# A two-block network on one core: attention's evictions reordered, the third norm's first tile on another engine, the norm's first chunks handed over singly

## The chip, the cores and the metric

One Trainium2 chip, of which the kernel uses one core. The metric is the device time in microseconds of one execution, the median of several. TensorE (PE) multiplies matrices out of SBUF into PSUM; VectorE (DVE), ScalarE (ACT) and GpSimd (POOL) work elementwise; SyncE (SP) issues most of the DMAs. Each engine runs its own instructions in order and meets the others at semaphores.

## The reference

The input is 256 tokens of width 1024, in float32. The first block has two layers. The first layer mixes with gated linear attention and an RWKV-7 recurrence, the second with latent attention (MLA) of 16 heads. Each layer ends in a feed-forward network, and each sublayer in a post-norm, so there are four layer norms. A second block follows, in which a condition vector modulates scales and shifts:

```python
def swiglu_ffn(x, w_gate_up, w_down):
    gu = x @ w_gate_up
    gate, up = gu[..., :FFN_HIDDEN], gu[..., FFN_HIDDEN:]
    return (jax.nn.silu(gate) * up) @ w_down

def layer_norm(x, g, b):
    xf = x.astype(jnp.float32)
    mu = xf.mean(-1, keepdims=True)
    var = jnp.square(xf - mu).mean(-1, keepdims=True)
    return ((xf - mu) * lax.rsqrt(var + LN_EPS) * g + b).astype(x.dtype)
```

The second block normalizes the rows by RMS, scales and shifts them by the modulation (a product of SiLU(c) with a 1024 by 6144 matrix), projects to queries, keys and values, attends with sinks and a relative bias (16 heads), adds a gated output, normalizes again, and ends with a 4096-wide squared-ReLU network.

## The kernel before

**Products.** Every large product is done with both factors split in a high and a low half (`mm3`, lines 443 to 446): high by high, high by low, low by high, three TensorE passes that accumulate in one PSUM bank.

**Weights.** All weight matrices are cut into pieces of up to 1 MB, in the order of their use (`pieces`). SyncE loads piece i into ring buffer i mod 3 as soon as piece i - 3 has left it (`sp_piece`, L434). ScalarE writes a piece's high half (`act_split`, L387), then VectorE the low half (`dve_split`, L400), which also frees the ring buffer. Split pieces go to three slots of their own; `ahead` says how far the splits run ahead of TensorE, two pieces. Among the pieces of the two feed-forward layers lie 24 of the modulation matrix (`w_ada`). TensorE doesn't use these: VectorE multiplies them with SiLU(c) and sums (`dve_modulation_piece`, L1738 and L1741), within `dve_split`, in the ring's order, and frees the buffer. The first such piece of a layer waits for the SiLU of c, which ScalarE does in `act_modulation_start` (L1718).

**Feed-forward.** `pe_ffn`, `act_ffn` and `dve_ffn` go over j = 0, 2, ..., 20, with two pieces each, g = 0 (gate) and g = 1 (up). The ring's order at the start of layer l is (j 0, g 0), (0, 1), modulation piece, (2, 0), (2, 1), modulation piece, (4, 0), (4, 1), modulation piece, and so on. The piece (0, 0) is split during the norm ahead. ScalarE's work in round j = 0 is the splits up to (2, 0) for g = 0, up to (2, 1) for g = 1, then the gate's SiLU.

**Norms.** Behind each norm TensorE transposes the two row tiles of XN into four banks, each with two chunks of 128 columns (`pe_transposed`, L532). VectorE scales and shifts the banks 0 and 2 (`dve_scaled`, L594 or L596), ScalarE the banks 1 and 3 (`act_scaled`, L571 or L573). ScalarE writes the high halves to XH (L581), VectorE the low halves to XL (L602), always for two chunks together. This happens six times: behind norms 0, 1 and 2, behind the RMS norm of MLA's compressed rows (tag cq), and for m0 and m1, the two modulated inputs of the second block. The consumers are `pe_pair` (first piece of a feed-forward layer and of w1) and `pe_rows` (min, mqb and va2).

**Norm 3** stands between the blocks. For row tile 0 `dve_residual` makes the statistics, `act_residual` normalizes to XN, and `pool_third` multiplies by the gain and adds the shift on GpSimd (L2318, L2322). For tile 1 `dve_third` does it all on VectorE (L2330, L2336). Then comes the RMS norm for m0 (`act_rms`, `dve_rms`).

**Attention.** `pe_attend`, `act_attend` and `dve_attend` run a pipeline over the heads with index i; head h = i - 3 is weighted in round i. In a round ScalarE first moves a finished group's output out of PSUM (L2158, every fourth head), then in MLA copies the turned queries and keys of an even head (L2163), then moves the transposed weights of head i - 3 (L2169, "moved"), for which TensorE's weighted sum waits (L2139), then takes the exponentials (L2175). `act_beside_mla` and `dve_beside_mla` put the splits of MLA's output weights (mout, four pieces) in set rounds: mout 4 in round 12 (VectorE in 13), mout 6 in round 17 (18). TensorE does the output products of mout 0 and 2 from round 15 on and of mout 4 and 6 behind the loop.

## Time and profile before

| what | us |
|---|---|
| median of three timed runs | 1136.97 |
| the three runs | 1138.66, 1131.41, 1136.97 |
| the profiled execution | 1133.92 |
| span of the profiled execution, first to last instruction | 1131.8 |

The profile is of one execution. "Busy" is the time in which an engine had an instruction at work. The number in brackets behind a row is the time that the engine stood idle before it, with the instruction that ended the wait. L numbers are lines of the kernel; many belong to helpers, so L444 to L446 stand for all split products, L387 and L400 for all weight splits.

### The profile page before, as it was taken

Reading aid. Unit: us, or ns where it says so; the run is one execution under the profiler, and the core shown is the slowest. Engines: PE = TensorE matmul, PEld = TensorE weight load, DVE = VectorE, ACT = ScalarE, POOL = GpSimd, SP = SyncE. Lnnn points to the kernel's source line nnn. Section 1 sums busy time; section 2 is a strip of 40 time slices with the busy share of each in tenths; the row PEclk is TensorE's granted clock in tenths of the full one; section 3 lists DMA queues with packets and bytes.
Section 4 is the critical chain, followed back from the end, with each engine's and each line's share of the span. In section 5 each row is a group of like instructions: output and inputs, shape, how many; then the busy total and the mean of one; then the engine's idle time right before and its main releaser. Section 6 shows DMA issues by size and latency. Waiting matters only on the chain.

```text
span 1131.8 us, 16907 instructions
## 1 busy us (share of the span) xinstructions
PE 1071.9 (95%) x7008; PEld 944.4 (83%) x7008; DVE 721.4 (64%) x1004; ACT 518.6 (46%) x742; POOL 134.8 (12%) x151
## 2 busy tenths in 40 slices
PE   7999999987999999899897999999799999999998
PEld 7888998877999988676676999988688778999886
DVE  4597863686776666677746676675755657666443
ACT  4452432354444343456645344443455656555332
POOL 2044841024000000500005000000200000000000
PEclk9899999898999999999999999999999998999999
DMA  9531011265786786336933886777353323555550
GB/s 301 162 104 57 1 39 38 76 222 189 259 297 216 259 305 224 131 123 148 202 113 103 299 283 221 242 290 272 100 184 115 112 75 106 187 185 186 193 186 38
DMA packets 113597, 193.67 MB, mean 171 GB/s; under 512 B 4690, under 2 KB 85089, under 8 KB 113394
## 3 DMA queue, kind: packets, MB, share of 16 engines
q1 hardware_dynamic: 109986, 180.18, 47.7%
q0 software_dynamic: 3248, 11.83, 4.8%
q8 instruction: 56, 0.92, 0.3%
q10 hardware_dynamic: 288, 0.59, 0.1%
q14 instruction: 19, 0.16, 0.0%
HBM read 188.39 MB, written 4.19 MB: 170 GB/s over the span
## 4 chain that ended last, share of the span: by engine, by line
PE 80%; DVE 10%; ACT 5%; DMA 3%; issue 2%; POOL 1%; DVEq 0%; SPq 0%; ACTq 0%; POOLq 0%
PE ps L444 22%; PE ps L446 21%; PE ps L445 21%; DMA ring<-in_ffn_w_gate_up_dram 2%; DVE ARR L400 2%; PE ps L2139 2%; PE ps L1281 2%; PE ps L1296 2%; PE ps L2124 2%; ACT ARR L387 1%; PE ps L2117 1%; DVE XL L602 1%; DVE AR L1218 1%; PE ps L1547 1%; PE ps L1504 1%
## 5 line engine op out<-in xcount | busy, mean ns | idle before, releaser
L400 DVE TENSOR_TENSOR ARR<-ring,ARR 128x2048 fp32r<-128x2048 f32 (+2 forms) x140 | 313.6, 2245 | 195.6 <-ACT ARR L387 195.5
L444 PE MATMUL ps<-XH,ARR 128*128 128x256 f32 x1240 | 356.0, 287 | 16.4 <-DVE ARR L400 6.6
L387 ACT ACTIVATE ARR<-ring 128x2048 fp32r<-128x2048 f32 (+2 forms) x141 | 263.5, 1875 | 200.6 <-PE ps L446 141.4
L445 PE MATMUL ps<-XL,ARR 128*128 128x256 f32 x1240 | 352.6, 284 | 0.0
L446 PE MATMUL ps<-XH,ARR 128*128 128x256 f32 x1240 | 352.3, 284 | 0.0
L444 PEld LDWEIGHTS ps<-XH,ARR 128*128 128x128 f32 x1240 | 237.6, 192 | 23.7 <-issue 19.0
L445 PEld LDWEIGHTS ps<-XL,ARR 128*128 128x128 f32 x1240 | 237.8, 192 | 0.5 <-issue 0.2
L446 PEld LDWEIGHTS ps<-XH,ARR 128*128 128x128 f32 x1240 | 237.5, 192 | 0.1
L444 PE MATMUL ps<-ARR 128*128 128x512 f32 x420 | 167.7, 399 | 5.0 <-DVE ARR L400 2.0
L446 PE MATMUL ps<-ARR 128*128 128x512 f32 x420 | 165.9, 395 | 0.0
L445 PE MATMUL ps<-ARR 128*128 128x512 f32 x420 | 165.8, 395 | 0.0
L444 PEld LDWEIGHTS ps<-ARR 128*128 128x128 f32 x420 | 78.8, 188 | 28.2 <-issue 5.1
L446 PEld LDWEIGHTS ps<-ARR 128*128 128x128 f32 x420 | 78.9, 188 | 19.0
L445 PEld LDWEIGHTS ps<-ARR 128*128 128x128 f32 x420 | 78.9, 188 | 18.1
L1741 DVE SCALAR_TENSOR_TENSOR AR<-ring,AR 128x1024 f32<-128x1024 f32 x42 | 53.9, 1283 | 1.1
L444 PE MATMUL ps<-ARR,XH 128*128 128x512 f32 x112 | 48.2, 431 | 5.1 <-DVE ARR L400 2.1
L1841 ACT ACTIVATE ARR<-XN 128x512 fp32r<-128x512 f32 x22 | 13.9, 632 | 76.3 <-DVE XN L1860 76.3
L678 POOL TENSOR_TENSOR X<-XN,GB 128x256 f32<-128x256 f32 x24 | 18.1, 781 | 244.6 <-ACT XN L644 244.6
L445 PE MATMUL ps<-ARR,XH 128*128 128x512 f32 x112 | 45.8, 409 | 0.0
L446 PE MATMUL ps<-ARR,XL 128*128 128x512 f32 x112 | 45.7, 408 | 0.0
L1264 POOL TENSOR_TENSOR AR<-AR,CST 128x512 f32<-128x512 f32 x28 | 38.4, 1404 | 18.7 <-DVE AR L1218 12.3
L2139 PE MATMUL ps<-AR 128*64 128x128 f32 x192 | 28.4, 285 | 6.7 <-ACT AR L2169 5.7
(352 smaller groups left out, 1236.3 us busy)
## 6 DMA issues: line engine op xcount, KB each, us to landing
ring<-in_ffn_w_gate_up_dram SPq DMA_DIRECT2D x44, 1024.0 KB, 5.8
ring<-in_w_dram SPq DMA_DIRECT2D x32, 1024.0 KB, 5.1
ring<-in_w_ada_dram SPq DMA_DIRECT2D x24, 1024.0 KB, 5.3
ring<-in_ffn_w_down_dram SPq DMA_DIRECT2D x22, 1024.0 KB, 5.1
ring<-in_even_w_in_dram SPq DMA_DIRECT2D x13, 1024.0 KB, 5.7
ring<-in_w_in_dram SPq DMA_DIRECT2D x9, 1024.0 KB, 5.3
ring<-in_mla_w_q_b_dram SPq DMA_DIRECT2D x6, 768.0 KB, 4.1
ring<-in_even_w_out_dram SPq DMA_DIRECT2D x4, 1024.0 KB, 4.9
```

The lines of the kernel that those rows point to most:

```text
L387: e.activation(split(i)[0], raw(i), ACT.Copy).then_inc(*up("hi", ("hi", i)))
L400: e.tensor_tensor(lo, raw(i), hi.bitcast(F32), ALU.subtract).then_inc(*up("lo", ("lo", i), ("raw free", i)))
L444: e.matmul(out, lhs[0], rhs[0], start=first, stop=False)
L445: e.matmul(out, lhs[0], rhs[1], start=False, stop=False)
L446: return e.matmul(out, lhs[1], rhs[0], start=False, stop=last)
L678: e.tensor_tensor(X[:, t, c], XN[:, t, c], GB[:, 0, c], ALU.mult).then_inc(*up("affine"))
L1264: e.tensor_tensor(level_part(lv, g), group(AAB, g), bc(f"lvl{lv}"), ALU.mult).then_inc(*up("level", ("al", lv, g)))
L1281: k = e.matmul(b[:, s * P:s * P + P], level_part(lv, g)[:, s, :], ident if lv == 0 else TI[:, 4 * g + s, :], start=True, stop=True)
L1296: k = e.matmul(b[:, s * P:s * P + P], w, w, start=True, stop=True)
L1741: k = e.scalar_tensor_tensor(acc, w[:, c, :], CSL[:, k0 + c:k0 + c + 1], acc, ALU.mult, ALU.add)
L2124: k = e.matmul(b[:, TILE[t]], A.q_of(i, t), A.k_of(i, P * (t + 1)), start=True, stop=True)
L2139: k = e.matmul(ps((A.tag, "o", g))[64 * (h % 2):64 * (h % 2) + 64, o + P * t:o + P * t + P], A.v_of(h, j), px[:, (t + j) * P:(t + j) * P + ...
```

## The change

1. `act_attend`: the eviction "moved" comes first in a round, ahead of the output's eviction and the head copy.
2. mout 4 is split in round 16 (VectorE 17), mout 6 in round 18 (19).
3. `act_scaled` and `dve_scaled`: chunks 0 and 1 are scaled, and made into high and low halves, one at a time; each has its own semaphore steps. ScalarE does the two high halves before it scales bank 1. `pe_pair` and, with `by_chunk`, `pe_rows` (min, mqb, va2) start with chunk 0 alone.
4. `act_ffn`: the SiLU of c comes behind both split calls of j = 0.
5. Norm 3, tile 0: `dve_third` on VectorE for both tiles; `pool_third` is gone. ScalarE does tile 0's RMS root ahead of tile 1's root of the norm, and its rows behind it.

```diff
+            for part in ((0,), (1,), (2, 3), (4, 5), (6, 7)):
+                e.wait_ge(*at((*xready(0), 0) if part == (0,) else xready(part[0] // 2)))
...
         def act_scaled(e, tag, dst, scale, shift, before, tf_before, part=(0, 1)):
+            if 0 in part:
+                for i in range(2):
+                    e.wait_ge(*at(("scaled", (tag, 0), i)))
+                    if i == 0:
+                        for step in before:
+                            e.wait_ge(*at(step))
+                    e.activation(dst[0][:, i, :], tf_half(0)[:, i, :], ACT.Copy).then_inc(
+                        *up("first", ("first", (tag, 0), i)))
...
+                if c == 0:
+                    for i in range(2):
+                        e.wait_ge(*at(("first", use, i)))
+                        e.tensor_tensor(dst[1][:, i, :], tf_half(0)[:, i, :], dst[0][:, i, :].bitcast(F32), ALU.subtract
+                                        ).then_inc(*up("rest", ("xt", use) if i else ("xt", use, 0)))
...
         def act_ffn(e, layer, i):
-            act_modulation_start(e, layer)
             for j in range(0, 22, 2):
                 u = UP[:, (j // 2) % 2, :]
                 for g in range(2):
                     act_split(e, ahead(("gu", layer, j, g), 0))
+                if j == 0:
+                    act_modulation_start(e, layer)
...
+            pe_rows(e, "min", 8, 1024, XT, xt_step("n1"), tail=2, by_chunk=True)
...
+            pe_rows(e, "mqb", 6, 1536, CT, xt_step("cq"), by_chunk=True)
...
+                if 0 <= i - LAG < 16:
+                    h = i - LAG
+                    e.wait_ge(*at(("full", (A.tag, "turn", h))))
+                    if h >= 2:
+                        e.wait_ge(*at((A.tag, "weighed", h - 2)))
+                    e.activation(A.px[:, h % 2], ps((A.tag, "turn", h))[:, 0:384], ACT.Copy).then_inc(
+                        *up("soft", (A.tag, "moved", h), ("free", (A.tag, "turn", h))))
                 g = leaving(i)
...
         def act_beside_mla(e, i, late):
-            if late and i in (8, 10, 12):
+            if late and i in (8, 10):
                 act_split(e, place_of["mout", i - 8])
-            elif late and i == 17:
-                act_split(e, place_of["mout", 6])
+            elif late and i in (16, 18):
+                act_split(e, place_of["mout", i - 12])
...
-            act_residual(e, 3, 0)
+            act_root(e, 3, 0)
             act_split(e, place_of["va2", 0])
+            act_rms_root(e, 0, 0, x_third)
             act_root(e, 3, 1)
-            for t in range(2):
-                act_rms(e, 0, t, x_third)
+            act_rms_rows(e, 0, 0)
+            act_rms(e, 0, 1, x_third)
...
-            dve_residual(e, ("down", 1), 3, x_after(2), 0)
+            dve_moments(e, ("down", 1), 3, x_after(2), 0)
+            dve_third(e, 0)
             dve_split(e, place_of["va2", 0])
-            dve_third(e)
-            for t in range(2):
-                dve_rms(e, 0, t, x_third)
+            dve_moments(e, ("down", 1), 3, x_after(2), 1)
+            dve_rms(e, 0, 0, x_third)
+            dve_third(e, 1)
+            dve_rms(e, 0, 1, x_third)
...
-            pool_third(e)
```

## Rows read from the trace of the kernel before

**Rows 1.** The page: busy time, share of the span and instructions per engine.
```profile
PE 1071.9 (95%) x7008; PEld 944.4 (83%) x7008; DVE 721.4 (64%) x1004; ACT 518.6 (46%) x742; POOL 134.8 (12%) x151
```

**Rows 2.** Windows, second attention: busy PE, PEld, DVE, ACT, POOL; clock, DMA, GB/s.
```profile
842.00:928.00 86.00, 86.00 (x553) 68.57 (x552) 47.74 (x157) 48.95 (x120) 0.00 (x0) 1.00 0.33 109
```

**Rows 3.** Chain of waits, first feed-forward layer's start: start us, length us, what.
```profile
263.95 1.28 ACT L1718
...
265.45 1.82 ACT ARR L387
...
267.30 2.30 DVE ARR L400
...
269.62 7.41 DMA ring<-in_ffn_w_gate_up_dram
...
277.05 1.93 ACT ARR L387
```

**Rows 4.** Timeline of TensorE in both feed-forward layers: start, length, [wait before].
```profile
269.74 0.35 PE L444 MATMUL ps<-XH,ARR 128*128 128x256 f32 x1 [1.06 <-DVE ARR L400]
...
300.61 0.36 PE L444 MATMUL ps<-XH,ARR 128*128 128x256 f32 x1 [0.86 <-DVE ARR L400]
...
641.75 0.36 PE L444 MATMUL ps<-XH,ARR 128*128 128x256 f32 x1 [0.80 <-DVE ARR L400]
```

**Rows 5.** Timeline of VectorE behind the second piece: modulation piece, then low half.
```profile
270.29 1.28 DVE L1741 SCALAR_TENSOR_TENSOR AR<-ring,AR 128x1024 f32<-128x1024 f32 x1
271.49 2.28 DVE L400 TENSOR_TENSOR ARR<-ring,ARR 128x2048 fp32r<-128x2048 f32 x1
```

**Rows 6.** DMA: lone load at 574; GpSimd's queue, 268 to 278; chain, second layer.
```profile
ring<-in_ffn_w_gate_up_dram SPq DMA_DIRECT2D x1, 1024.0 KB, 5.0
...
q0 software_dynamic: 508, 1.82, 51.7%
...
621.74 8.89 DMA ring<-in_ffn_w_gate_up_dram
```

**Rows 7.** First attention: the weighted sum's group with its waits; timeline rows.
```profile
L2139 PE MATMUL ps<-AR 128*64 128x128 f32 x96 | 14.5, 289 | 6.7 <-ACT AR L2169 5.7 <-DVE AR L2214 1.0
...
572.90 0.48 PE L2139 MATMUL ps<-AR 128*64 128x128 f32 x1 [2.26 <-ACT AR L2169]
...
570.09 1.90 ACT L387 ACTIVATE ARR<-ring 128x2048 fp32r<-128x2048 f32 x1
...
595.11 0.69 DVE L2225 TENSOR_TENSOR XL<-ps,XH 128x512 fp32r<-128x512 f32 x1 [3.69 <-ACT XH L2158]
...
594.38 0.50 PE L444 MATMUL ps<-ARR,XH 128*128 128x512 f32 x1
```

**Rows 8.** Windows at the lower clock; columns as in rows 2.
```profile
572.70:575.60 2.90, 2.70 (x12) 2.35 (x13) 1.77 (x2) 1.02 (x5) 0.00 (x0) 0.50 0.05 5
814.90:818.10 3.20, 2.98 (x13) 2.58 (x14) 1.03 (x4) 1.61 (x4) 0.00 (x0) 0.50 0.00 0
...
937.80:947.60 9.80, 7.58 (x34) 7.21 (x35) 5.72 (x12) 7.00 (x12) 0.00 (x0) 0.50 0.00 1
```

**Rows 9.** Timeline of TensorE: first product of w1, behind m1.
```profile
943.69 0.55 PE L444 MATMUL ps<-XH,ARR 128*128 128x256 f32 x1 [1.59 <-DVE XL L602]
```

**Rows 10.** Timeline around norm 3; the DVE row of 932.91 is without GpSimd beside it.
```profile
805.91 2.53 POOL L2318 TENSOR_TENSOR X<-XN,GB 128x512 f32<-128x512 f32 x2 [186.17 <-ACT XN L644]
808.52 3.47 POOL L2322 TENSOR_TENSOR X<-X,GB 128x512 f32<-128x512 f32 x2
...
810.98 2.23 DVE L2336 SCALAR_TENSOR_TENSOR X<-XN,STAT,GB 128x512 f32<-128x512 f32 x2
...
817.09 1.60 PE L532 MATMUL ps<-CST,XN 128*128 128x128 f32 x8 [0.19 <-ACT XN L2360]
...
828.20 0.50 PE L444 MATMUL ps<-ARR,XH 128*128 128x512 f32 x1 [0.17 <-DVE ARR L400]
...
932.91 1.41 DVE L2581 SCALAR_TENSOR_TENSOR X<-XN,STAT,X 128x512 f32<-128x512 f32 x2
```

More of the change, by code:

```diff
@@ L452, in pe_pair @@
             e.wait_ge(*at(("lo", w)))
-            for c in range(0, 8, 2):
-                e.wait_ge(*at(xready(c // 2)))
+            for part in ((0,), (1,), (2, 3), (4, 5), (6, 7)):
+                e.wait_ge(*at((*xready(0), 0) if part == (0,) else xready(part[0] // 2)))
                 for h in range(2):
-                    for c_ in (c, c + 1):
+                    for c_ in part:
                         k = mm3(e, b[h][:, h * 256:h * 256 + 256], cut(hilo, ALL, c_, slice(h * P, h * P + P)),
@@ L503, in pe_rows @@
                     e.wait_ge(*at(("lo", w, 0) if w == gate else ("lo", w)))
+                if by_chunk and t == k0 == 0:
+                    for c in range(k0, k1):
+                        e.wait_ge(*at(xready(c // 2) if c else (*xready(0), 0)))
+                        for j, (o, m) in enumerate(parts):
+                            if c == 0 and before[t, j] is not None:
+                                e.wait_ge(*at(("free", before[t, j])))
+                            mm3(e, ps((tag, t, j))[:, 0:m], cut(xT, ALL, c, slice(0, P)),
+                                cut(hilo, ALL, c - k0, slice(o, o + m)), c == 0, False)
+                    continue
                 for j, (o, m) in enumerate(parts):
@@ L574, in act_scaled @@
                 k.then_inc(*up("first", ("scaled", use), ("free", use)))
-                for v in range(2):
+                for v in range(1 if c == 2 else 0, 2):
                     use = (tag, c // 2 - 1 + v)
                     e.wait_ge(*at(("scaled", use)))
-                    if c == 2 and v == 0:
-                        for step in before:
-                            e.wait_ge(*at(step))
                     e.activation(dst[0][:, c - 2 + 2 * v:c + 2 * v, :], tf_half(v), ACT.Copy).then_inc(
@@ L596, in dve_scaled @@
                         k = e.tensor_scalar(y, x, scale(c + i), shift(c + i), ALU.mult, ALU.add)
-                k.then_inc(*up("rest", ("scaled", use), ("free", use)))
-                for v in range(2):
+                    if c == 0:
+                        k.then_inc(*up("rest", ("scaled", use, i), *([("free", use)] if i else [])))
+                if c == 0:
+                    for i in range(2):
+                        e.wait_ge(*at(("first", use, i)))
+                        e.tensor_tensor(dst[1][:, i, :], tf_half(0)[:, i, :], dst[0][:, i, :].bitcast(F32), ALU.subtract
+                                        ).then_inc(*up("rest", ("xt", use) if i else ("xt", use, 0)))
+                if c:
+                    k.then_inc(*up("rest", ("scaled", use), ("free", use)))
+                for v in range(0 if c else 1, 2):
                     use = (tag, c // 2 + v)
@@ L2344, in x_gated, with act_rms_root @@
             return ("x gated", 0, t, h)
[L2346 to L2347 removed]
+        def act_rms_root(e, k, t, x_ready):
+            acc = STAT[:, t, 0:1]
             if t == 0:
```

50 lines of the change are left out of this document (17 added, 33 removed).

## The prediction

> **What bounds the kernel now.** I read the page first, then the stretches around each place that the change touches. The page says TensorE is busy for 95% of the span, VectorE for 64%, ScalarE for 46% [rows 1]; so time is only to be had where TensorE stands still, or runs at its lower clock. The stretches show where that is. The second attention leaves TensorE no idle time at all: 86.00 us busy of 86.00 [rows 2]. The first attention has short waits, counted below. The rest stands around the norms. A reader should then follow the chain of waits out of the first norm before a feed-forward layer: table load for the SiLU, two ScalarE high halves, VectorE's low half, a DMA of 7.41 us that starts the moment that low half frees a ring buffer, then ScalarE again [rows 3]. In that chain the weights, not the activations, decide when TensorE gets its second and later pieces.
>
> **The change part by part.**
>
> *SiLU of the modulation later.* At present ScalarE loads the SiLU table (1.28) and does the small SiLU before it takes high halves: 1.49 us from the table load to the next split [rows 3]. TensorE's second weight piece started at 269.74 after a wait of 1.06 [rows 4]. Moving the SiLU away brings that second piece forward by 1.5, in the other layer too. But the new place is behind *both* rounds of splits of j = 0, and the last of these, gate/up piece (j 2, g 1), has first to be loaded: it needs the ring buffer of piece (0, 1), whose DMA was issued at 269.62, after that piece's low half, and landed at 277.03 [rows 3]. VectorE's queue behind the low half of (0, 1) holds the first modulation piece, which waits for this SiLU, and behind it the low half of (2, 0), TensorE's third piece [rows 5]. So a new ring of waits: low half (0, 1), DMA, high half (2, 1), table load and SiLU, modulation piece, low half (2, 0), TensorE. Its length:
>
> DMA. A lone 1 MB load into the ring landed after 5.0 us. At the layer's start it doesn't run alone: gain rows and gate rows issued by GpSimd still move 1.82 MB between 268 and 278, and the load of this place took 7.41, in the other layer 8.89 [rows 3, 6]. Those two had two more ring loads beside them for their later half; now none is issued until this one has landed. GpSimd's transfers stay. I take 6.9, nearer to the loaded case than to the lone one, with 5.0 and 8.9 as bounds.
>
> After landing: high half 1.93, table and SiLU 1.49, modulation piece 2.0 (from the end of the low half at 269.6 to 271.49), low half 2.29 [rows 3, 5]: 7.7. From low half to low half 14.6 us, while one piece is 5.7 us of TensorE ((300.61 less 269.74, less waits of 1.9 in sum, over five pieces [rows 4], rounded). The second piece's low half ends at 269.6 less 1.5 plus 0.3 (the norm's own chain gets longer, next part), 268.4; the third's at 283.0, instead of TensorE starting it at 275.4 (269.74 and 5.7). TensorE stands 8.9 us. The three waits, 1.9 us, that it had until 300.61 (the last one 0.86 [rows 4]) go into this one, since the DMA queue catches up: after the restart ring loads come faster than 5.7 us apiece. That leaves 7.6 less 1.9, +5.7. In the other layer the low half of piece two ended at 621.74, when the DMA was issued [rows 6], and now ends at 620.1 (this norm's chain lengthens by less); that of piece three ends 14.6 later, 634.7. The fifth piece starts two pieces, 11.4, after the third: 646.1, where before it was 641.75 [rows 4], +4.4. The stall itself then costs clock: after a wait of 2.26 the first attention ran at 0.50 granted, the 1.2 GHz level, for 2.9 us [rows 7, 8]. A wait four times as long will do the same, for 1.6 us of lost work in each layer. The two layers together: 5.7 + 4.4 + 3.2 = +13.3. With DMAs of 5.0 it is 9.5; with 7.41 and 8.89, 15.8; with twice the slow stretch 3.2 more, 19.
>
> The Trainium skill (TensorE: Matmul & The Clock Gate, Part 1) says that the throttled state is the default and that activity releases it. The trace agrees at the waits above. Were it not so, the sum for the two layers would be 10.1.
>
> *First pair of chunks one at a time.* ScalarE used to scale chunks 2 and 3 at once, beside VectorE's scaling. It now first waits for VectorE's chunk 0 and makes two small high halves, so chunks 2 to 7 come 0.3 to 0.4 later, an estimate from halved passes. Chunk 0 is ready about 1.2 us earlier: a half-width high and low half in place of full-width ones, and no wait for chunk 1. Who gains? In front of the feed-forward layers nobody, since the second weight piece sets the time (done above). Behind the second norm TensorE is busy with a modulation product until the chunks are there; VectorE's longer queue delays the next low half: +0.3. In the rotary/query projection the start comes earlier, but the following low halves, queued behind the norm, each arrive 0.7 later: +0.2. Ahead of the last layer TensorE waited 1.59 for the chunk until 943.69 [rows 9]; of the 1.2 gained, 0.4 goes back to the second weight piece: -0.7. Sum -0.2, bounds -2 and +1.5.
>
> *Attention's evictions first; two splits later.* In the first attention the weighted sum waited 6.7 us in total, in six places, the last and longest 2.26 at 572.90 [rows 7]. Each time ScalarE had done another head's copy or an output eviction first, and before the last a 1.90 us split of the output weights at 570.09 [rows 7]. With the eviction first, and that split moved to where TensorE has long projection products, all go but about 0.9 of the first, where the exponentials themselves are late. Gain 5.8, and 1.45 for the slow stretch behind the 2.26 [rows 8]. Given back: the last output weights' split moves to the end of ScalarE's loop; VectorE then does it behind the output's low half at 595.11: 595.11 + 0.69 + 2.29 = 598.0 [rows 7]. TensorE, from 594.38 on with 12 products of 0.233, wants it at 597.2: +0.85. VectorE's output low halves now collide with its head copies, 0.3 each time: +0.6. Net -5.8. Bounds: -7.3 if neither comes, -2.5 if only the moved split counts. In the second attention the order changes nothing, as TensorE has no gap there [rows 2].
>
> *Third norm's tile 0 on VectorE.* GpSimd's two pairs go: 2.53 + 3.47, from 805.91 to 811.99, and ScalarE's affine pass before them [rows 10]. VectorE instead does one 1024-wide pass and two 512-wide ones. The price of two 512-wide ones is 2.23 beside GpSimd and 1.41 without it [rows 10]; GpSimd is idle now, so I take 1.41, and as much for the wide one. Tile 0 is ready at about 806.9 (it was 812.0), tile 1's moments start 0.65 late, but its two last passes are 0.8 cheaper, so tile 1 stands at 813.2 as before. What then ends last is tile 1's half square, which ScalarE did behind tile 0's rows and can now do 1.6 us earlier; the last transposes go from 817.09 [rows 10] to 815.45. The second weight piece of the projection waits for VectorE (828.20 [rows 10]) and gives 0.45 back by the chunk order: -1.2. TensorE then stands 3 us ahead of it, which may cost half a slow stretch: -0.6, bounds -1.6 and +0.8.
>
> The Trainium skill (SBUF — State Buffer, Who interferes with whom) says that VectorE and GpSimd share one port pair and that the loser waits out the whole instruction. The 2.23 against 1.41 agrees with it. At 2.23 the third norm's tile 0 would be 0.8 later, and the sum 0.2 higher.
>
> **Sum.** 13.3 - 0.2 - 5.8 - 0.6 = +6.7 us. The profiled execution took 1133.92 with a span of 1131.8; the three timed runs 1131.41, 1136.97 and 1138.66. These four have a mean of 1135.2, and that is the base I use, as they scatter by as much as the effect: 1135.2 + 6.7 = 1142.
>
> **Rivals.**
> *A. The new stall is longer.* The load takes 7.41 and 8.89 as before, the clock stays low for two stretches: 19 instead of 13.3, +12.4 in all, 1147.6, and with the attention's lower bound 1151. For it: those DMA times were measured at this very place. Against: two loads fewer run beside it.
> *B. TensorE's clock turns it round.* One mechanism: the shorter waits keep the clock at 2.4 GHz where it fell to 1.2 (the last norm's transposes and first products, the third norm's transposes, the restart in both layers). Worth about 4.0, 1.4 and 3.2 by half of the slow working time [rows 8]: 6.7 - 8.6 = -1.9, 1133. It decides from about three quarters of these 8.6 us on. Against: the 8.9 us stall is far longer than the waits that let the clock fall.
> *C. The attention gains only the moved split.* Head copies and softmax come later in exchange, VectorE becomes what is waited for: -2.5 instead of -5.8, +10, 1145. For it: the page of the profile has VectorE, not ScalarE, as what TensorE waits for in 1.0 of the 6.7 us [rows 7]. Against: the other 5.7 are ScalarE's.
> *D. The moved SiLU stalls nothing,* because the first modulation piece finds its scale in time. The ring of waits would have to be no longer than the 5.7 us of a piece; at the least load time seen it is 12.7. Then -1.5 a layer, 1126. I see no way to it.
>
> **How the numbers follow.** Forecast 0.60, A 0.17, B 0.09, C 0.11, D 0.03. A change of this kernel smaller than about 1% (11 us) can't be told from none. The forecast, B and C lie within 1%; A reaches over it for most of its chance, and so does the edge of C: slower 0.20, same 0.76, faster 0.04. The range goes from 1134, which takes in B's upper half, to 1150, where A begins to run out.
>
> **What would show it.** In the profile after: in both feed-forward layers TensorE waits 7 to 10 us for the low half ahead of the third piece, VectorE's first modulation piece waits for ScalarE's SiLU, and the DMA queue stands idle for some 5 us after one landed load; in the first attention the waits of the weighted sum fall from 6.7 to under 2; GpSimd has no work in the third norm, and the two VectorE passes there take about 0.7 each. The prediction is wrong if the stall is under 5 us or if TensorE gets its second piece no earlier.

## The result and the profile after

| | before | after |
|---|---|---|
| median of the timed runs, taken in turn on one chip | 1135.44 us | 1144.29 us |
| lowest and highest of them | 1131.41, 1138.66 | 1143.16, 1148.13 |
| ratio to before, with its 95% interval | 1 | 1.0105 (1.0078 to 1.0131) |
| span of the profiled execution | 1131.8 us | 1145.7 us |
| mean granted clock of TensorE in that execution | 0.976 | 0.965 |

The kernel became slower by 12 us by the ratio, 9 us by the medians. The sign is that of the forecast (+6.7 us, 1142), and the size lies within its range, but by the ratio it is nearly twice what was said: the forecast is 2 us under the median and 5 us under what the ratio makes of its base (1135.2 x 1.0105 = 1147.1). Rival A had 1147.6. The new stall is dearer than predicted, the chunk order costs time, and the third norm gives back more.

The page of the profile after: first the busy time per engine, then rows of the span in 40 equal slices, in tenths (TensorE's busy share, its granted clock):

```profile
PE 1076.5 (94%) x7008; PEld 949.2 (83%) x7008; DVE 724.2 (63%) x1012; ACT 518.8 (45%) x747; POOL 128.4 (11%) x147
...
PE   7999999895999999899898699999999999999998
...
PEclk9899998997999999999998799999989998999999
```

No engine got busier to speak of: TensorE has 4.6 us more than in [rows 1], VectorE 2.8, GpSimd 6.4 less. What is to be seen are the two holes of TensorE's row, a 5 in the tenth slice (258 to 286 us) and a 6 in the 23rd (630 to 659 us). The clock's row has a 7 in both slices. They are the starts of the two feed-forward layers.

The timeline of TensorE in the profile after shows them: the first product of the second and of the third weight piece in each layer, with the wait in the brackets.

```profile
269.84 0.36 PE L444 MATMUL ps<-XH,ARR 128*128 128x256 f32 x1 [0.75 <-DVE ARR L400]
...
285.40 0.55 PE L444 MATMUL ps<-XH,ARR 128*128 128x256 f32 x1 [9.64 <-DVE ARR L400]
...
627.29 0.36 PE L444 MATMUL ps<-XH,ARR 128*128 128x256 f32 x1 [0.68 <-DVE ARR L400]
...
644.63 0.55 PE L444 MATMUL ps<-XH,ARR 128*128 128x256 f32 x1 [11.43 <-DVE ARR L400]
```

In place of waits of about 1 us [rows 4] TensorE waits 9.64 and 11.43 us for the low half of its third weight piece. The product behind such a wait takes 0.55 instead of 0.36 us: the clock is down. The chain of waits, first layer and then second (start, length, what), names every link of the ring that the prediction described:

```profile
267.40 2.31 DVE ARR L400
269.72 7.70 DMA ring<-in_ffn_w_gate_up_dram
277.49 1.88 issue
279.37 1.28 ACT L1743
280.66 0.22 ACT AR L1743
280.97 0.77 DVE AR L1763
281.80 1.17 issue
282.96 2.30 DVE ARR L400
...
285.40 0.55 PE ps L444
```

```profile
627.17 9.48 DMA ring<-in_ffn_w_gate_up_dram
636.72 1.88 issue
638.60 1.28 ACT L1743
...
640.21 0.77 DVE AR L1763
...
642.20 2.30 DVE ARR L400
```

Beside [rows 3], where the ring's load is followed by the next high half and nothing else: now a high half (shown as 1.88 of "issue"), the table load and the SiLU (L1743), the modulation piece (L1763 and 1.17 us behind it) stand between the load and the low half for which TensorE waits. VectorE's own row says the same:

```profile
280.97 0.75 DVE L1763 TENSOR_SCALAR AR<-ring,AR 128x1024 f32<-128x1024 f32 x1 [11.28 <-ACT AR L1743]
...
640.21 0.75 DVE L1763 TENSOR_SCALAR AR<-ring,AR 128x1024 f32<-128x1024 f32 x1 [13.06 <-ACT AR L1743]
```

VectorE stands 11.28 and 13.06 us for the SiLU of c, a vector of 1024 numbers. From 277.5 to 283.0 no DMA packet moves either: the ring has three buffers, and all wait for VectorE.

**Where the time went, by stages.** The span can be cut at points that TensorE reaches in both kernels, the first transposes behind each norm, the first product of a certain kind. The stages' lengths, read from TensorE's timeline:

| stage | before | after | difference |
|---|---|---|---|
| start to the transposes of the mixer's last norm (code not touched) | 225.7 | 225.6 | -0.1 |
| to the transposes behind norm 0 | 28.0 | 28.9 | +0.9 |
| first feed-forward layer, to its column product in round 14 | 92.4 | 100.4 | +8.0 |
| to the transposes behind norm 1 | 112.7 | 112.7 | 0 |
| norm 1 and `min`, to the transposes of cq | 31.7 | 33.2 | +1.5 |
| `mqb`, to the first score | 46.1 | 48.2 | +2.1 |
| first attention, to the transposes behind norm 2 | 70.1 | 64.7 | -5.4 |
| second feed-forward layer, to its column product | 91.9 | 101.7 | +9.7 |
| to the column product of norm 3 | 108.8 | 108.8 | 0 |
| norm 3 and projections, to the second attention's first score | 40.8 | 38.9 | -1.9 |
| to the end | 283.6 | 282.7 | -0.9 |

The two feed-forward starts cost 17.7 us, the attention gives 5.4, the third norm 1.9, and the other stages add 3.5 (+0.9, +1.5, +2.1, -0.9 and -0.1). The sum is 13.9, the difference of the two spans.

Of these 3.5 most is the clock, as the other kernels' profiles of the same stages show. From the mixer's last norm to the transposes behind norm 0 seven profiles take 28.0 to 28.1 us and have no stretch at the 1.2 GHz level there; the six that have one, after among them, take 28.7 to 29.1. `min` takes 31.7 in the two profiles where the low stretch falls ahead of TensorE's wait for the second weight piece, and 33.1 to 33.5 in the eleven where one begins about at the wait's end, whatever was changed. Only in `mqb` is a part of the edit's own, see the chunk order below.

How far one profile's stage can be trusted: with the SiLU at its old place the first feed-forward layer's stage is 91.3 to 92.4 us in six profiles, the second's 91.7 to 92.7. A difference of 1 us between two single profiles is no finding.

### The profile page after: what moved, and what is told of

Read it like the earlier page. It is cut to its first block, busy times and chain, and to the rows that moved or that the text cites. A ratio compares the mean times of both kernels' runs of the same rounds, so it can differ in the third digit from the quotient of the medians.

```text
span 1145.7 us, 16916 instructions
## 1 busy us (share of the span) xinstructions
PE 1076.5 (94%) x7008; PEld 949.2 (83%) x7008; DVE 724.2 (63%) x1012; ACT 518.8 (45%) x747; POOL 128.4 (11%) x147
## 4 chain that ended last, share of the span: by engine, by line
PE 82%; DVE 10%; ACT 4%; DMA 2%; issue 2%; DVEq 0%; SPq 0%; ACTq 0%
PE ps L444 23%; PE ps L445 22%; PE ps L446 22%; PE ps L2165 2%; DVE ARR L400 2%; PE ps L1306 2%; PE ps L2150 2%; PE ps L1321 2%; DMA ring<-in_ffn_w_gate_up_dram 1%; PE ps L2143 1%; ACT TF L593 1%; ACT ARR L387 1%; DVE AR L1243 1%; DVE XL L627 1%; PE ps L1572 1%
## 5 line engine op out<-in xcount | busy, mean ns | idle before, releaser
L444 PEld LDWEIGHTS ps<-ARR 128*128 128x128 f32 x420 | 79.8, 190 | 28.5 <-issue 4.2
L446 PEld LDWEIGHTS ps<-ARR 128*128 128x128 f32 x420 | 79.6, 189 | 18.9
L445 PEld LDWEIGHTS ps<-ARR 128*128 128x128 f32 x420 | 79.9, 190 | 18.1
L1867 ACT ACTIVATE ARR<-XN 128x512 fp32r<-128x512 f32 x22 | 13.9, 632 | 88.2 <-DVE XN L1886 88.2
L444 PEld LDWEIGHTS ps<-ARR,XH 128*128 128x128 f32 x112 | 22.7, 203 | 14.7 <-DVE ARR L400 6.5
```

Of the source, the lines that this page charges most:

```text
L444: e.matmul(out, lhs[0], rhs[0], start=first, stop=False)
L445: e.matmul(out, lhs[0], rhs[1], start=False, stop=False)
L446: return e.matmul(out, lhs[1], rhs[0], start=False, stop=last)
```

## The experiments

All ratios are to the kernel before, which ran in turn with each of three groups of kernels, each group on one chip, so the ratios compare better than the medians do. Intervals are 95%.

### The SiLU of c between the two splits

```diff
                 for g in range(2):
                     act_split(e, ahead(("gu", layer, j, g), 0))
-                if j == 0:
-                    act_modulation_start(e, layer)
+                    if j == g == 0:
+                        act_modulation_start(e, layer)
```

> The whole change, but the SiLU of the condition stands between the two split calls of j = 0: behind the high half of piece (2, 0), ahead of that of (2, 1), for which ScalarE waits on a DMA. Theory (ring of waits: the SiLU stands behind a load): TensorE's wait ahead of the third piece falls from 9.65 and 11.43 us to under 1 in both layers, the rest of the change keeps its gain; about 7 us under the kernel before, 1128. Rival (the load is slow, whatever ScalarE does): the waits stay above 5 us and the time stays above 1138.

Measured: 1127.54 us, ratio 0.9953 (0.9935 to 0.9971). The two feed-forward starts take 91.1 and 91.6 us instead of 100.4 and 101.7. TensorE's timeline in this kernel:

```profile
273.18 0.36 PE L444 MATMUL ps<-XH,ARR 128*128 128x256 f32 x1 [0.75 <-DVE ARR L400]
...
634.96 0.36 PE L444 MATMUL ps<-XH,ARR 128*128 128x256 f32 x1 [2.71 <-DVE ARR L400]
```

The first row is the second piece of the first layer, the second row the fourth piece of the second layer. There is no wait before the third piece at all. In the first layer the second piece comes 15.3 us behind the transposes of norm 0 instead of 16.0, the gain of the later SiLU less what the norm lost in this execution. Whether it reaches the end of the stage can't be told: 91.1 and 91.6 stand beside 91.3 to 92.4 and 91.7 to 92.7 with the SiLU at its old place, and in the second layer the fourth piece waits 2.71. The stall is therefore not made by moving the SiLU away from the norm, but by moving it behind a split whose piece can only be loaded once VectorE goes on.

### The whole change with the SiLU where it was

```diff
         def act_ffn(e, layer, i):
+            act_modulation_start(e, layer)
             for j in range(0, 22, 2):
...
-                if j == 0:
-                    act_modulation_start(e, layer)
```

> The whole change, but the SiLU of the condition stands ahead of all splits, as in the kernel before. Theory: no long wait ahead of the third piece; the second piece again 1.5 us later than with the SiLU moved, so 2 to 3 us slower than the version with the SiLU between the splits: 1131, some 4 us under the kernel before. If the moved SiLU had been a gain in itself, this would be slower than the kernel after (1144).

Measured: 1127.87 us, ratio 0.9948 (0.9926 to 0.9970); the stages are 92.4 and 91.9 us, as before. The 2 to 3 us that this kernel was expected to be slower than the one above didn't show. So the other three edits together are worth -5.9 us (0.5% of 1135; the prediction's -0.2 - 5.8 - 0.6 is -6.6), and the moved SiLU costs 1.57 points, 17.8 us, which is also what the stages give (17.7). The prediction had 13.3.

### Only the SiLU moved

```diff
         def act_ffn(e, layer, i):
-            act_modulation_start(e, layer)
             for j in range(0, 22, 2):
...
+                if j == 0:
+                    act_modulation_start(e, layer)
```

> The kernel before with nothing changed but the place of the SiLU, behind both split calls of j = 0. Theory: the whole loss of the two layers and nothing else, 15 to 18 us by the milestones of the two traces, 1151 to 1153. My prediction's size for it was 13.3, 1148. Rival (the loss comes from the chunk order or elsewhere): under 5 us.

Measured: 1153.98 us, ratio 1.0188 (1.0166 to 1.0210), 21 us, 3 more than expected. TensorE's timeline:

```profile
283.21 0.55 PE L444 MATMUL ps<-XH,ARR 128*128 128x256 f32 x1 [10.59 <-DVE ARR L400]
...
647.82 0.55 PE L444 MATMUL ps<-XH,ARR 128*128 128x256 f32 x1 [10.71 <-DVE ARR L400]
```

The stall belongs to this edit alone, and needs neither the chunk order nor the rest. In the first layer it is 0.95 longer than in the whole change, and the ring's load is as well: 8.90 against 7.70. The two starts cost 8.9 and 9.5 us against before, 18.4 in sum; where the rest of the 21 lies isn't shown.

The load's length goes with how soon it follows GpSimd's. GpSimd issues its first gain row at 265.45 before, at 265.94 in the whole change and at 263.69 here; the ring's load follows 4.17, 3.78 and 2.64 us later and takes 7.41, 7.70 and 8.90. Moving the SiLU away brings the load forward and GpSimd's transfers not: the edit itself makes its load longer.

### What makes the load long

The load of the ring's next piece had taken 5.0 alone, and 7.41 and 8.89 in its place [rows 3, 6]. In this kernel GpSimd issues the DMAs of the next norm's gain rows and gate rows only when the SiLU of c is done, behind the load in question:

```diff
             for t in range(2):
                 e.wait_ge(*at(("x", i, t)))
+            if i in (0, 2):
+                e.wait_ge(*at(("csl", i // 2)))
             pool_gain_rows(e, i + 1)
```

> The whole change, and GpSimd issues the gain and gate rows of each feed-forward layer only after the SiLU of the condition, so that the load of piece (2, 1) has the DMA engines to itself. Theory (GpSimd's 2.1 MB hold up the load): the load falls from 7.7 and 9.5 us to about 5.2, TensorE's waits from 9.65 and 11.43 to about 7; 5 to 7 us under the kernel after, 1138. Rival (1 MB takes that long in itself at this place): waits and time as after, 1144.

Measured: 1146.55 us, ratio 1.0113 (1.0091 to 1.0135), no different from the change; 5 to 7 us less had been expected. The chain of waits and TensorE's timeline of its first layer:

```profile
266.48 5.09 DMA ring<-in_ffn_w_gate_up_dram
...
279.43 12.16 DMA ring<-in_ffn_w_gate_up_dram
```

```profile
279.55 0.55 PE L444 MATMUL ps<-XH,ARR 128*128 128x256 f32 x1 [7.04 <-DVE ARR L400]
...
296.00 0.36 PE L444 MATMUL ps<-XH,ARR 128*128 128x256 f32 x1 [2.82 <-DVE ARR L400]
```

The load falls from 7.70 to 5.09, the lone time, and the wait by the same 2.6, from 9.64 to 7.04. In the second layer the load falls from 9.48 to 6.99 and the wait from 11.43 to 8.94. So GpSimd's transfers made the load longer by 2.6 and 2.5 us. In the first layer that is all of the surplus over 5 us. In the second 2 us stay, with no packet of GpSimd's beside the load. The DMA view of that load, 623.4 to 630.4 us (packets, MB, share of the 16 DMA engines):

```profile
q1 hardware_dynamic: 1040, 1.05, 45.9%
q8 instruction: 1, 0.02, 1.8%
```

One packet of kind "instruction" took 1.8% of 16 engines for 7.0 us, which is 2.0 us of one engine, and the last 0.05 MB of the load arrive between 627.9 and 629.9. That this packet holds them up is argued from the equal lengths and not tested. GpSimd's transfers, for their part, have to run at some time: now they meet the next loads, of which one takes 12.16, and TensorE waits 2.82 (2.53 in the other layer) two pieces later. The stages are 100.8 and 101.3 us, against 100.4 and 101.7. The gain is given back whole.

How the engines share can be read from the DMA view of the profile after, 269.8 to 274.5 us, while both queues have work (packets, MB, share of the 16 DMA engines):

```profile
q0 software_dynamic: 410, 1.47, 78.5%
q1 hardware_dynamic: 305, 0.31, 18.8%
```

GpSimd's queue (q0) has packets of 3.6 KB, the ring's queue (q1) of 1.0 KB. By the shares a packet of q0 holds its engine for 0.14 us and one of q1 for 0.05. The numbers of packets are near each other, the bytes are not: the ring gets 0.31 of 1.78 MB. The Trainium skill (DMA: Bandwidth & Descriptors, Queues, rings and completion order) says that a DMA engine takes turns between its queues packet by packet; if the packets of this view are those that the page means, the queue with the larger ones gets the larger part while both have work. 410 against 305 packets and 78.5% against 18.8% agree with it roughly, though no run here changed the packets' size.

### Does the stall cost clock beside its own length?

Two kernels keep TensorE at work in the stall, with extra products (float32, 128x512) ahead of the third piece, which nothing reads. The first had 18 and 20 of them, the second 9 and 10:

```diff
                         b = bank(e, tag)
+                        if (j, g) == (2, 0):
+                            for n in range(9 + layer):
+                                e.matmul(b, cst("ones"), CST[:, 0:512], start=True, stop=True)
                         e.wait_ge(*at(("lo", w)))
```

> The kernel after, with 18 (first layer) and 20 (second) plain float32 products of 128x128 by 128x512, which nothing reads, on TensorE ahead of the wait for the third piece, in that piece's own bank; by 0.46 us apiece from the modulation's product at full clock, 8.3 and 9.2 us. Theory (the long wait costs clock besides its own length): the granted clock stays at the 2.4 GHz level over the stall, the third piece runs at full rate, 1.4 and 2.7 us come back: 1140. Rival (the length of the wait is all that costs): 1144 as the kernel after, or more where the filler runs past the wait.

Measured: 1154.31 us, ratio 1.0183 (1.0156 to 1.0210). The size of a product was wrong by half. TensorE's timeline:

```profile
274.86 15.61 PE L1837 MATMUL ps<-CST 128*128 128x512 f32 x36
```

18 products are 36 records of 0.43 us, 15.6 us instead of 8.3, and outlast the stall by some 5 us. As a test of the time this run says nothing. With half as many:

> The change, with 9 and 10 extra float32 products of 128x512 ahead of the third piece in the two feed-forward layers; nothing reads their result, they only keep TensorE at work for 7.8 and 8.7 us (0.87 each by e5_filler's trace) of the 9.6 and 11.4 us that it otherwise stands. If the stall costs clock as well as its own length, the lower clock behind it goes: 1.4 and 2.7 us less than the change by its trace, in sum 4.1, so about 1.007 of before where the change has 1.0105. If the lower clock behind the stall is only the chance that falls somewhere in every run, the time stays at the change's 1.0105.

Measured: 1144.66 us, ratio 1.0102 (1.0075 to 1.0130). The windows of the restart, for this kernel and for the change as it is (busy time of TensorE, its weight loads, VectorE, ScalarE, GpSimd; granted clock, DMA share, GB/s):

```profile
278.00:288.00 10.00, 8.65 (x26) 3.99 (x25) 3.88 (x3) 3.95 (x5) 0.00 (x0) 1.00 0.23 70
636.00:650.00 14.00, 11.63 (x62) 7.98 (x61) 9.25 (x8) 4.58 (x6) 0.00 (x0) 1.00 0.46 149
```

```profile
278.00:288.00 10.00, 2.60 (x12) 2.63 (x13) 6.99 (x5) 3.39 (x5) 0.00 (x0) 0.50 0.37 121
636.00:650.00 14.00, 5.37 (x25) 5.40 (x26) 9.03 (x8) 4.58 (x6) 0.00 (x0) 0.52 0.46 147
```

With TensorE kept at work the clock stays at 1.00 (2.4 GHz) where it otherwise is at 0.50 (1.2 GHz). The two stages are shorter by 1.4 and 1.7 us (99.0 and 100.0 us). The three kernels with the stall (after, SiLU alone, late GpSimd DMAs) have the low clock behind it in both layers, six times of six; the two with extra products never, in four. The lower clock behind the stall thus comes from TensorE's standing still and costs 3.1 us in the two layers; the prediction had 3.2. The whole kernel doesn't show it: 1.007 was expected. Its profile is 1.4 us shorter, since it lost 3.0 us more than the change in the first stage, in code that is the same; and the two ratios, 1.0102 and 1.0105, can't tell 3 us from none (each is known to 0.3%, 3 us). So the clock's price is shown by the stages, and not by the time.

The Trainium skill (TensorE: Matmul & The Clock Gate, Part 1) calls the throttled state the default, which activity releases. The windows agree: same code and same stretch, 0.50 after standing still and 1.00 after dummy work.

### The attention's part alone

The kernel before with the eviction "moved" first in a round, and with mout 4 and 6 in rounds 16 and 18 (items 1 and 2 of the change's list):

> The kernel before with the attention's part alone: the eviction for the weighted sum first in a round, the two splits of the output weights later. My prediction's size is -5.8, 1127.6 against 1133.4; the milestones of the traces of before and after give -5.5. Rival C (head copies and softmax come later in exchange): the weighted sum's waits stay above 3 us and the gain is at most 2.5.

Measured: 1128.14 us, ratio 0.9959 (0.9938 to 0.9981), -4.6 us. And with item 1 alone, the splits in their old rounds:

> The kernel before with the eviction 'moved' first in each round of the attention and nothing else; the output weights' splits stay in rounds 12 and 17. By the prediction the waits of the weighted sum behind head copies and output evictions go (about 3.5 of 6.7 us) and the last one, behind the split at 570, stays at 2 or so with its slow stretch: 3 us faster than before, against 4.6 for both together (f1_attention). By rival C the order gains nothing, since other evictions come later in exchange: no change, and the moved split made all the 4.6 us.

Measured: 1129.59 us, ratio 0.9982 (0.9962 to 1.0003), -2.0 us, hardly told from none. The groups of the weighted sum, over both attentions, show more (busy, mean ns | waits): first the kernel before, then with the order alone, then after.

```profile
L2139 PE MATMUL ps<-AR 128*64 128x128 f32 x192 | 28.4, 285 | 6.7 <-ACT AR L2169 5.7 <-DVE AR L2214 1.0
```

```profile
L2139 PE MATMUL ps<-AR 128*64 128x128 f32 x192 | 28.2, 284 | 3.2 <-ACT AR L2159 2.9
```

```profile
L2165 PE MATMUL ps<-AR 128*64 128x128 f32 x192 | 27.7, 281 | 1.9 <-ACT AR L2185 1.0 <-DVE AR L2225 0.7
```

The order takes 3.5 of the 6.7 us away. What it leaves is mainly the first wait of 1.00 and one of 1.92, behind the split of mout 4:

```profile
567.57 0.67 PE L2139 MATMUL ps<-AR 128*64 128x128 f32 x3 [1.92 <-ACT AR L2159]
```

The moved split takes that one. By stages the first attention lasts 70.1 us before, 66.8 with the order, 64.2 with both: 3.3 and 2.6. That answers rival C, which left only the moved split, 2.5: the waits that the order removes don't come back elsewhere.

The lower clock behind the last wait doesn't come each time. Five profiles have that wait: before, order alone (1.92) and SiLU alone have the low clock behind it; the chunk order alone and the third norm alone, with the attention's code as before, have not. TensorE's row and the window behind it (columns as in [rows 2]) in the third norm's kernel:

```profile
577.07 0.87 PE L2139 MATMUL ps<-AR 128*64 128x128 f32 x6 [2.26 <-ACT AR L2169]
...
577.00:580.40 3.40, 3.33 (x25) 2.65 (x26) 3.06 (x8) 1.39 (x6) 0.00 (x0) 1.00 0.17 45
```

The same wait of 2.26 as in [rows 7], and the clock stays at 1.00 where [rows 8] has 0.50. The attention takes 68.7 and 68.8 us in these two, 70.1 before, 71.7 with the SiLU alone, where the low clock lasts twice as long. So the slow stretch is worth 1.4 us, as predicted, but only where it comes; the eight profiles with order and moved split have 64.2 to 64.9. Against 68.7 the attention's part is worth about 4 us, against 70.1 over 5; the timed 4.6 lies between.

### The chunk order alone

Item 3 of the change's list on the kernel before; nothing else.

> The kernel before with the chunk order alone, behind all six norms. My prediction's size is -0.2, with the second weight piece's low half 0.3 later where the SiLU stands in front; so no change, within 2 us. By the milestones of after: +3 if the low half behind the second norm and the slow clock behind it belong to this order, 0 if the slow stretch there is chance (the version with the SiLU back in front had none). If a shorter wait for the first chunk did bring time of its own, it would be 4 us faster.

Measured: 1136.44 us, ratio 1.0035 (1.0015 to 1.0054), 4 us slower, where no change was expected. Its one profile has a span of 1129.9 us at a mean clock of 0.985, the highest of all, and so shows no loss as a whole. The stages of all thirteen profiles say where the order costs, seven with it and six without.

`mqb` takes 46.0 to 46.1 us in the six profiles without the chunk order, and 46.6 to 48.2 in the seven with it. TensorE's start there, before and after:

```profile
494.94 0.47 PE L444 MATMUL ps<-ARR 128*128 128x512 f32 x1 [1.59 <-DVE ARR L602]
```

```profile
504.25 0.47 PE L444 MATMUL ps<-ARR 128*128 128x512 f32 x1 [0.64 <-issue]
...
509.49 0.50 PE L444 MATMUL ps<-ARR 128*128 128x512 f32 x1 [1.51 <-DVE TF L611]
```

The first chunk alone saves 0.95 of the wait, and then TensorE waits 1.51 for VectorE (L611, the scaling of a later bank), where it didn't wait before: +0.6. In four of the seven that is all (46.6 to 46.7). In the other three, after among them, a low stretch of 3.4 us lies near the stage's end and makes it 48.2; no profile without the chunk order has one there, but three of seven prove no cause.

Norm 3 and the projections (`va2`) take 37.9 and 38.1 us with the new norm and without the chunk order, 38.6 to 38.9 with both: 0.5 to 1.0. Behind m1, where the prediction had -0.7, the rest of the kernel takes 192.5 to 193.2 us with the order and 192.7 to 193.4 without: TensorE starts 0.3 to 0.7 us earlier and waits again a little later, 0.48 us after and 0.63 and 0.93 in this kernel. `min` (+1.6 in this kernel's profile) and the feed-forward starts show no cost: kernels without the order have the same there. In sum the stages give 1.1 to 1.6 us, and 1.5 more where the low stretch in `mqb` comes; the rest of the 4.0 isn't found.

### The third norm alone

Item 5 on the kernel before.

> The kernel before with the third norm's tile 0 on VectorE alone. My prediction's size for it with the chunk order was -0.6, -1.2 without a slow stretch; the traces of before and after are 1.9 apart there, with the chunk order in it. Without the chunk order VectorE reaches the second weight piece 0.45 earlier: -1.5 to -2.5. Rival (VectorE becomes the bound, since it now does both tiles): tile 1's moments late by 0.65 and more, no gain or a loss.

Measured: 1128.93 us, ratio 0.9963 (0.9944 to 0.9983), -4.2 us. Stages: norm 3 and the projections 37.9 us against 40.8, so -2.9 (within the interval of the 4.2, and more than the 1.5 to 2.5 that were expected). With the chunk order beside it, in the whole change, 38.9.

### Without the chunk order

From the first experiment's kernel, with item 3 undone:

```diff
-            pe_rows(e, "min", 8, 1024, XT, xt_step("n1"), tail=2, by_chunk=True)
+            pe_rows(e, "min", 8, 1024, XT, xt_step("n1"), tail=2)
```

and in the same way `mqb`, `va2`, `pe_pair`, `act_scaled` and `dve_scaled`, all as before the change.

> Attention's order and splits, the third norm on VectorE, and the SiLU between the two splits of j = 0 (as in e1_between); the norms' first chunks stay in pairs as before. If the chunk order costs what f2_chunks showed (some 4 us), this kernel is faster than e1_between (0.9953) and stands near 0.992, 9 us under before. If that cost was only the chance of where the slow stretches fell, it stands at 0.995 to 0.996, like e1_between: by the stages (0.2 to 1 us for the chunks) no more than 1 us apart.

Measured: 1124.23 us, ratio 0.9939 (0.9916 to 0.9963), the best of all kernels: 7 us under before and, by the ratios, 19 under the change. Against the same kernel with the chunk order (0.9953, measured in another group) it is 1.6 us better, which the intervals don't separate, but which is the size that the stages of `mqb` and `va2` give. The chunk order thus brings nothing, and costs between 0 and some 4 us by the times, 1.1 to 1.6 by the stages.

## Why the prediction was right, point by point

The side was right for the reason given. The size has luck in it: the forecast's +6.7 stands against +11.9 by the ratio and +13.9 between the two profiles, and its nearness to the median of 1144.29 comes from a median that is 3 us under what the ratio makes of the base. By stages, with the predicted terms in front: the two feed-forward starts +13.3 and +17.7, the attention -5.8 and -5.4, the third norm -0.6 and -1.9, all else -0.2 (the chunk order) and +3.5. The errors are +4.4, +0.4, -1.3 and +3.7, so they don't cancel.

**What bounds the kernel** was right: what was won or lost lies where TensorE stands still or runs at 1.2 GHz.

**The ring of waits was right**, link by link, and with it the side of the result. Counted from low half to low half, it was predicted at 14.6 and is 15.5 in the first layer (269.71 to 285.26) and 17.3 in the second (627.16 to 644.50). Nearly all of the difference is the load's term; what follows the landing takes 7.8 in both layers, where 7.7 was said. I took 6.9 for the load, reasoning that two ring loads fewer would run beside it; it took 7.70 and 9.48, not less than the 7.41 and 8.89 before. What counts is how close behind GpSimd's transfers the load is issued, and the edit brings it closer: the kernel with the late GpSimd DMAs shows 2.6 and 2.5 us of theirs. Of rival A the longer load came, and of the clock's cost only the forecast's 3.2: its sum for the two layers, 19, is nearer to the measured 17.7 than the forecast's 13.3. That its total, 1147.6, is what the ratio makes of the base is chance, since the chunk order and the clock of untouched code are in it.

**The stall's net cost was mis-sized.** The terms were +5.7 and +4.4, and 3.2 for the clock: 13.3. Measured are 17.7 by the stages. Where the 4.4 us come from:

- the load, 0.8 in the first layer and 2.6 in the second: 3.4. This is the term that was mis-sized, for the reason above.
- the second piece, 0.5 in the first layer. From the transposes of norm 0 to the end of its low half it was to take 14.7 us and takes 15.2 (269.71 less 254.55). With the SiLU alone moved it takes 14.4 (266.32 less 251.97) against 15.9 before: 1.5 earlier, as predicted. The 0.8 between is not the chunk order's, for which 0.3 was set: the kernel with the late GpSimd DMAs has the chunk order and the moved SiLU and takes 14.4 too. What differs is for 0.5 of the 0.8 one pass of VectorE. After, the transposes run at the 1.2 GHz level, the pass is later and falls beside GpSimd's (262.13, L708); in the other kernel it is ahead of it. After, then late GpSimd DMAs:

```profile
262.19 1.22 DVE L627 TENSOR_TENSOR XL<-TF,XH 128x512 fp32r<-128x512 f32 x1 [0.73 <-ACT XH L598]
```

```profile
259.48 0.69 DVE L627 TENSOR_TENSOR XL<-TF,XH 128x512 fp32r<-128x512 f32 x1 [0.54 <-ACT XH L598]
```

- the rest, 0.5, is -0.6 in the first layer and +1.1 in the second, no more than single profiles of a stage differ by.

**The clock behind the stall** was right in sum: 3.2 predicted, 3.1 by the stages with and without extra products. It isn't 1.6 in each layer, though: by the windows the products between 636 and 650 us lose 2.7 us (half of their 5.37), but with the clock at 1.00 TensorE waits 1.00 for the ring a little later, so 1.7 are left. That row of the kernel with 9 and 10 products:

```profile
656.93 0.36 PE L444 MATMUL ps<-XH,ARR 128*128 128x256 f32 x1 [1.00 <-DVE ARR L400]
```

Rival B, in which the clock turns the result round, falls. The restarts run at 0.50 and 0.52. Behind the third norm the windows after have 0.50 for 6.8 us (831.0 to 837.8), and before for 6.7 (814.8 to 818.1 and 821.6 to 825.0). Only at the last norm, its largest part, is the low stretch shorter, 6.8 us (953.9 to 960.7) instead of 10.1 (937.7 to 947.8), and the other kernels have 6.8 to 10.2 there without the chunk order, 3.4 to 10.2 with it. Little of that reaches the time: from m1's transposes to the end it is 192.5 us after and 193.4 before, of a range of 192.5 to 193.4 over all profiles.

**The attention** was right: -5.8 predicted, -5.4 by the stages. The waits of the weighted sum fall from 6.7 to 1.9, where "under 2" was said, and what was to be given back is in the 5.4. Both causes have about the size that the waits gave them: 3.3 by the order, 2.6 by the split with its clock. The clock's 1.45 is right as a size, but two profiles of five with the wait don't have it, so it belongs to some executions and not to the kernel. Rival C falls.

**The third norm was mis-sized**: -0.6 predicted with a bound of -1.6, measured -1.9 in the whole change, and -2.9 without the chunk order. VectorE's passes in the profile after are about as priced, 0.71 each for the narrow ones, and 1.28 for the wide one where 1.41 was taken:

```profile
820.50 1.28 DVE L2343 SCALAR_TENSOR_TENSOR XN<-XN,STAT,GB 128x1024 f32<-128x1024 f32 x1
...
821.89 1.42 DVE L2349 SCALAR_TENSOR_TENSOR X<-XN,STAT,GB 128x512 f32<-128x512 f32 x2
...
827.70 1.42 DVE L2349 SCALAR_TENSOR_TENSOR X<-XN,STAT,GB 128x512 f32<-128x512 f32 x2
```

```profile
831.38 0.90 PE L543 MATMUL ps<-CST,XN 128*128 128x128 f32 x3 [2.67 <-ACT XN L2376]
...
842.99 0.50 PE L444 MATMUL ps<-ARR,XH 128*128 128x512 f32 x1 [0.94 <-DVE ARR L400]
```

Counted from the column product (807.45 before, 824.13 after), tile 0 stands 5.4 us earlier (5.1 predicted), tile 1 at 4.99 instead of 5.76, where "as before" was said, and the last transposes start at 7.25 instead of 9.64 [rows 10]: 2.4 earlier, predicted 1.6. So the step that was mis-sized is tile 1, which gained 0.8 where nothing was expected. The second weight piece comes at 18.9 instead of 20.7, and its wait for VectorE, 0.94, which the kernel with the third norm alone doesn't have, is what the chunk order costs here: 0.5 to 1.0 us by the stages, predicted 0.45. The 0.6 for half a slow stretch didn't come. Without GpSimd beside them two narrow passes were priced at 1.41 and took 1.42.

**The chunk order was mis-sized** the other way: -0.2 predicted, bounds -2 and +1.5, measured +4.0 alone (1.7 to 6.1), 1.6 with the other edits beside it, 1.1 to 1.6 by the stages. The step that failed is the gain ahead of the last layer: 0.7 was taken for it and nothing arrives at the end, since the later chunks and the second weight piece are waited for instead. In `mqb` the cost is 0.6 where 0.2 was said, in `va2` 0.5 to 1.0 where 0.45 was. How much of the 4.0 beyond that is a chance of the clock isn't settled.

The single parts, each alone against before, give 21.3 + 4.0 - 4.6 - 4.2 = +16.5, all at once +11.9. Each is uncertain by 2 to 3 us, the difference of 4.6 therefore by some 5: the times show neither that the parts add nor that they don't. The -5.9 for three parts and the +17.8 for the SiLU sum to the +11.9 by the way they are taken, not as a finding.

## What to carry to other kernels

Before a small operation is moved behind a larger one on an in-order engine, ask what the larger one waits for, and whether that wait can only end after the small one: here a SiLU of 1.5 us, put behind a split that needed a fresh load, closed a ring of buffer, DMA, ScalarE and VectorE of 15 to 17 us; one split further forward it costs nothing. A load on such a ring is priced with all transfers that share the DMA engines at that moment, and putting those off only moves the collision. A measured edit is best taken back alone from the full change as well as done alone: three of these edits gain 5.9 us together, and the fourth hid it. And a transfer that starts earlier can take longer, when what it then meets hasn't moved with it.

## What the runs showed of the hardware

**TensorE's clock falls where nothing waits, and not at the same places each time.** Windows of the profile after, in a part of the kernel that the change doesn't touch:

```profile
32.50:36.00 3.50, 3.50 (x9) 1.01 (x8) 3.43 (x5) 1.19 (x2) 0.00 (x0) 0.96 0.65 195
36.00:42.50 6.50, 6.50 (x23) 4.91 (x23) 4.97 (x10) 2.40 (x2) 0.00 (x0) 0.50 0.48 157
```

TensorE is busy in all of these 10 us, yet between 36.0 and 42.5 its clock is at 0.50, the 1.2 GHz level. What it did before the fall was mostly long products of 512 columns (0.56 us each, 9 instructions in 3.50 us). The same products, from 33.0 to 37.3 us in the profile of the attention's part alone, are followed by no fall: that profile has 1.00 from 34.9 to 41.4. The first 225 us, the same code in all thirteen profiles, last from 222.6 to 229.6 us. Near the two ends the mean granted clock over the first 222 us reads 0.98 (attention alone) and 0.95 (third norm alone). Waits differ in the same way: behind those of 1.9 to 2.3 us in the attention the clock fell in three profiles of five, behind those of 7.0 us and more in six of six.

So 7 us of one profile against another can be the clock in code that nobody changed, as much as the whole forecast of this case. Single stages between two points have to be compared, not spans, and over more than one profile.

**Two queues share the DMA engines by packets more than by bytes.** While both had work, GpSimd's queue with 3.6 KB packets moved 1.47 MB and the ring's with 1.0 KB packets 0.31 MB. A 1 MB load took 5.1 us without GpSimd's transfers (late GpSimd DMAs, first layer) and 7.7 with them.

**A float32 product of 128x512**, as the extra ones above, took 0.87 us of TensorE, in two records of 0.43.
